# An opening that reads x^T from the host's layout and multiplies both first weight blocks in float32

## What is computed

```python
def rms_norm(x, g, eps=NORM_EPS):
    xf = x.astype(jnp.float32)
    y = xf * lax.rsqrt(jnp.mean(xf * xf, axis=-1, keepdims=True) + eps)
    return (y * g.astype(jnp.float32)).astype(x.dtype)

def swiglu(x, wg, wu, wd):
    return (jax.nn.silu(x @ wg) * (x @ wu)) @ wd

x = x + 0.5 * swiglu(rms_norm(x, ffn1_norm[l]), ffn1_wg[l], ffn1_wu[l], ffn1_wd[l])
```

## Time and profile before

| | |
|---|---|
| median of 3 runs | 858.0 us (857.75 to 858.19) |
| profiled execution | 858.39 us, span of its instructions 856.6 us |
| TensorE busy | 848.3 us, 99% of the span |
| VectorE, ScalarE, GpSimd busy | 637.6, 524.8 and 59.6 us |
| chain that ended last | 98% TensorE |
| mean granted TensorE clock | 0.998 |
| moved by DMA | 162.47 MB, mean 190 GB/s |

### The profile page before, as it was taken

The page is one execution under the profiler, slowest core; times in us unless marked ns, Lnnn a source line. Parts: engine busy times, 40 slices in busy tenths (PEclk is TensorE's granted clock), DMA queues, the critical chain, the costliest instruction groups (busy, mean ns, idle before and its releaser), DMA issues.

```text
span 856.6 us, 11976 instructions
## 1 busy us (share of the span) xinstructions
PE 848.3 (99%) x4775; PEld 738.0 (86%) x4775; DVE 637.6 (74%) x788; ACT 524.8 (61%) x738; POOL 59.6 (7%) x65
## 2 busy tenths in 40 slices
PE   9999999999999999999999999999999999999997
PEld 8988888888889898888888887888888898888885
DVE  5999999987698656765466468758777677877873
ACT  6677777766575544653554356548666665576772
POOL 0022222210000000000000000100000001000001
PEclk9999999999999999999999999999999999999999
DMA  8976566554544655576456545586655655853501
GB/s 271 351 238 201 179 197 197 194 159 158 204 148 141 204 193 177 172 252 231 155 165 231 195 148 187 195 284 224 203 197 193 210 179 168 262 177 108 191 1 50
DMA packets 123991, 162.47 MB, mean 190 GB/s; under 512 B 3864, under 2 KB 111136, under 8 KB 123808
## 3 DMA queue, kind: packets, MB, share of 16 engines
q1 hardware_dynamic: 122320, 154.89, 55.0%
q0 software_dynamic: 1312, 6.29, 2.2%
q10 hardware_dynamic: 304, 0.53, 0.2%
HBM read 160.65 MB, written 1.05 MB: 189 GB/s over the span
## 4 chain that ended last, share of the span: by engine, by line
PE 98%; DVE 1%; ACT 0%; POOL 0%; issue 0%; POOLq 0%; DVEq 0%
PE pAcc L448 23%; PE pG L392 9%; PE pU L392 9%; PE pAcc L392 7%; PE pG L395 5%; PE pR L392 5%; PE pU L395 5%; PE pM L392 4%; PE pAcc L395 3%; PE pR L395 2%; PE pAcc L428 2%; PE pAcc L427 2%; PE pAcc L426 2%; PE pM L395 2%; PE pG L509 1%; PE pM L428 1%
## 5 line engine op out<-in xcount | busy, mean ns | idle before, releaser
L326 DVE TENSOR_TENSOR lo<-raw,hi 128x2048 fp32r<-128x2048 f32 x131 | 298.5, 2288 | 52.7 <-ACT hi L321 52.7
L321 ACT ACTIVATE hi<-raw 128x2048 fp32r<-128x2048 f32 x140 | 265.5, 1907 | 18.4 <-PE pAcc L428 5.6
L392 PE MATMUL pG<-xT,hi 128*128 128x512 f32 x336 | 83.7, 391 | 0.0
L392 PE MATMUL pU<-xT,hi 128*128 128x512 f32 x320 | 80.2, 392 | 0.0
L448 PE MATMUL pAcc<-hi,h_hi 128*128 128x512 f32 x240 | 74.8, 393 | 0.0
L448 PE MATMUL pAcc<-lo,h_hi 128*128 128x512 f32 x240 | 74.2, 390 | 0.0
L448 PE MATMUL pAcc<-hi,h_lo 128*128 128x512 f32 x240 | 74.0, 389 | 0.0
L392 PEld LDWEIGHTS pG<-xT,hi 128*128 128x128 f32 x336 | 62.1, 188 | 13.0 <-issue 0.7
L1110 ACT ACTIVATE h_hi<-h 128x512 fp32r<-128x512 f32 x28 | 17.7, 633 | 81.2 <-PE pAcc L448 75.4
L392 PEld LDWEIGHTS pU<-xT,hi 128*128 128x128 f32 x320 | 57.5, 189 | 10.3
L1629 DVE TENSOR_TENSOR h_lo<-h,h_hi 128x512 fp32r<-128x512 f32 x28 | 19.3, 689 | 46.5 <-ACT h_hi L1110 46.5
(11 more groups left out here) (505 smaller groups left out, 1639.3 us busy)
## 6 DMA issues: line engine op xcount, KB each, us to landing
raw<-in_a_w_in SPq DMA_DIRECT2D x24, 1024.0 KB, 5.3
raw<-in_ffn_wd SPq DMA_DIRECT2D x22, 1024.0 KB, 5.3
raw<-in_ffn_wg SPq DMA_DIRECT2D x21, 1024.0 KB, 5.3
raw<-in_ffn_wu SPq DMA_DIRECT2D x21, 1024.0 KB, 6.2
raw<-in_w_in SPq DMA_DIRECT2D x16, 1024.0 KB, 5.5
raw<-in_a_w_out SPq DMA_DIRECT2D x8, 1024.0 KB, 5.0
raw<-in_w_kv SPq DMA_DIRECT2D x8, 1024.0 KB, 5.5
raw<-in_b_w_qz SPq DMA_DIRECT2D x8, 1024.0 KB, 5.6
```

Of the source, the lines that this page charges most:

```text
L321: act.activation(HI[n % NHL][:, :], RAW[n % NRAW][:, :], ACT.Copy).then_inc(S["hi"], 1)
L326: dve.tensor_tensor(LO[n % NHL][:, :], RAW[n % NRAW][:, :], HI[n % NHL][:, :].bitcast(f32), ALU.subtract).then_inc(S["lo"], 1)
L392: pe.matmul(v3(bank[:, :], 2), wh[:, k, w], x4[:, :, k, :], start=(k == 0), stop=False, skip_group_check=True)
```

## The change

x is no longer transposed by TensorE. The host hands over x^T, features on the partitions, with the gain's 8 columns ahead of it (`x_t`, 128 by 8 + 2048), loaded in four pieces (`load_x_t`). Both first blocks are multiplied in float32 for both tiles; block 1 is not split. ScalarE squares x^T and writes each square 8 elements from the last, so that the 8 chunks of one token and partition are neighbours; VectorE sums these eights (`sum_first`, output 128 x 128), TensorE multiplies the sum with a column of 1/1024 (`mean_square`), and VectorE adds eps (`variance_first`). The rows of x, which the residual needs much later, are loaded by one transfer of 1 MB (`load_x`) ahead of block 8. Tile 1's up product is now unnormed too, so its half of h is multiplied by its power. The small tables for the bias are laid out by the host, and their two transfers stand behind block 3. The core of the diff:

```diff
         def load_block(sp, n):
-            if n >= NRAW:
-                sp.wait_ge(S["lo"], n - NRAW + 1)
-            if n in (NRAW, NRAW + 1):
-                sp.wait_ge(S["used"], 1)
+            if n in (NRAW, NRAW + 1):
+                sp.wait_ge(S["used"], n - NRAW + 1)
+            elif n > NRAW:
+                sp.wait_ge(S["lo"], n - NRAW + 1)
...
+        def load_x_t(engine, b):
+            c = slice(KD + b * 512 if b else 0, KD + (b + 1) * 512)
+            engine.dma_start(XRAW[:, c], T["x_t"][:, c]).then_inc(S[f"x_in{b}"], 16)
+
+        def load_x(sp):
+            sp.wait_ge(S["x_sum"], 2)
+            sp.dma_start(v3(X[:, :], NT), T["x"][0].rearrange("(t p) c -> p t c", p=P)).then_inc(S["x_rows"], 16)
...
+        def mean_square(pe, t):
+            pe.wait_ge(S["x_sum"], t + 1)
+            pe.matmul(VAR[t], SSQ[:, t * P:(t + 1) * P], MEAN, start=True, stop=True).then_inc(S["x_var"], 1)
...
         def pe_start(pe):
-            busy(pe, 7)
-            x_transposes(pe, 0, 0)
-            pe.wait_ge(S["gain0"], 16)
-            pe.transpose(ACC[1][:, 0:KD], G8, IDENT[0:KD, 0:KD]).then_inc(S["gc_ps"], 1)
-            x_transposes(pe, 0, 1)
+            busy(pe, 9)
...
-            pe.wait_ge(S["lo"], 2)
-            pe.wait_ge(S["xt_lo"], 3)
-            to_tokens(pe, 1, U, XT, (1,), half_way=4).then_inc(S["used"], 1)
+            first_block(pe, 1, U, 1, range(0, KD)).then_inc(S["used"], 1)
+            pe.wait_ge(S["xt_lo"], 4)
...
         def xt_first(dve, b):
-            dve.wait_ge(S["xt_ps"], b + 1)
-            dve.tensor_tensor(xf(b), v3(XBANK[b][:, :], 4), fbc(GC[:, 4 * (b % 2):4 * (b % 2) + 4], P),
+            dve.wait_ge(S["x_in0"], 16)
+            if b:
+                dve.wait_ge(S[f"x_in{b}"], 16)
+            dve.tensor_tensor(xf(b), x_raw(b), fbc(GC[:, 4 * (b % 2):4 * (b % 2) + 4], P),
                               ALU.mult).then_inc(S[f"xf{b}"], 1)
+
+        def squares(t):
+            return XSQ[:, t * D:(t + 1) * D].rearrange("p (c k) -> p c k", k=KD)
+
+        def square_first(act, b):
+            act.wait_ge(S[f"x_in{b}"], 16)
+            half = slice(4 * (b % 2), 4 * (b % 2) + 4)
+            act.activation(squares(b // 2).rearrange("p c k -> p k c")[:, half, :], x_raw(b), ACT.Square).then_inc(S["ssq"], 1)
+
+        def sum_first(dve, t):
+            dve.wait_ge(S["ssq"], 2 * t + 2)
+            dve.tensor_reduce(SSQ[:, t * P:(t + 1) * P], squares(t), AX.X, ALU.add).then_inc(S["x_sum"], 1)
+
+        def variance_first(dve, t):
+            dve.wait_ge(S["x_var"], t + 1)
+            c = RS_COL["norm", 0, t][0]
+            dve.tensor_scalar(ST[:, c:c + 1], VAR[t], 1e-6, None, ALU.add).then_inc(S["var"], 1)
...
-                        dve.tensor_tensor(H[:, BC:512], U[:, BC:512], SA[:, BC:512], ALU.mult).then_inc(S["h"], 1)
+                        k = RS_COL["norm", 0, 1][0]
+                        dve.scalar_tensor_tensor(out=H[:, BC:512], in0=U[:, BC:512], scalar=ST[:, k:k + 1], in1=SA[:, BC:512],
+                                                 op0=ALU.mult, op1=ALU.mult).then_inc(S["h"], 1)
...
-                if b == ("ffn1", "gate", 3):
+                if b == ("ffn1", "gate", 2):
+                    load_x(sp)
+                elif b == ("ffn1", "gate", 3):
```

More of the change, by code:

```diff
@@ L57 @@
 NRAW, NHL = 4, 4
+UNSPLIT = 2
 LEAD = 3
@@ L101 @@
     "hi": "hi parts of weight blocks", "lo": "lo parts of weight blocks", "used": "weight blocks multiplied",
-    "x_in00": "x of token tile 0 loaded, its first half", "x_in01": "its second half",
-    "x_in10": "x of token tile 1 loaded, its first half", "x_in11": "its second half",
+    "x_in0": "x^T of token tile 0 loaded, its first half", "x_in1": "its second half",
+    "x_in2": "x^T of token tile 1 loaded, its first half", "x_in3": "its second half",
+    "x_sum": "squares of a token tile summed over the chunks of features",
+    "x_var": "and over the features of a chunk", "x_rows": "x loaded", "mean": "1 / D",
     "first0": "first half of weight block 0 loaded", "first1": "first half of weight block 1 loaded",
@@ L106 @@
     "xf2": "that of token tile 1, first half", "xf3": "its second half",
-    "gc_ps": "first gain by features in a bank", "gc": "and in SBUF", "rb": "powers of the first norm along columns",
-    "hi_first": "hi part of the first half of block 1",
+    "rb": "powers of the first norm along columns",
     "const_in": "lambda vectors, subln gain and DFT matrices loaded",
@@ L296, in load_half @@
                 full[n] if half else S[f"first{n}"], 16)
[L300 to L314, removed]
         def hi(act, n):
@@ L511, in first_block @@
             return end
[L513 to L519, removed]
         def power_row(pe, t):
@@ L1045, in rows @@
             dve.wait_ge(S["rsqrt"], RS_ORDER.index(what) + 1)
-            dve.wait_ge(S[f"gain{g % 2}"], 16 * (g // 2 + 1))
+            dve.wait_ge(S[f"gain{g % 2}"], 16 * (g // 2 + g % 2))
             for n in range(2):
@@ L1631, in dve_turn @@
         def dve_turn(dve, r, g, q, ph, scale, x, n):
+            if r == 0:
+                dve.wait_ge(S["x_rows"], 16)
             lo_half(dve, n + 1, 0)
@@ L2508, in _ @@
             pool.memset(HALF[:, :], -0.5).then_inc(S["half"], 1)
+            pool.memset(MEAN, 1.0 / D).then_inc(S["mean"], 1)
             pool.wait_ge(S["ident"], 1)
@@ L2512, in _ @@
             pool.wait_ge(S["half"], 1)
+            pool.wait_ge(S["mean"], 1)
             power(pool, ("norm", 0, 0))
@@ L2541, in _ @@
         def _(act):
-            load_x(act, 0, 1)
-            load_gain_first(act)
+            load_x_t(act, 1)
             act.wait_ge(S["half"], 1)
             warm(act, ACT.Square)
[L2546 to L2549, removed]
+            for b in range(4):
+                square_first(act, b)
+            warm(act, ACT.Silu)
             xt_hi_first(act, 0)
             xt_hi_first(act, 1)
-            hi_half(act, 0)
-            hi_half(act, 1)
-            warm(act, ACT.Silu)
             xt_hi_first(act, 2)
@@ L2605, in _ @@
             pe.wait_ge(S["ident"], 2)
+            pe.wait_ge(S["mean"], 1)
             pe_ffn(pe, "ffn1", 0, 1)
@@ L2626 @@
     arrays["dft_tok"] = np.ascontiguousarray(dft.transpose(1, 0, 2)).astype(np.float32)
-    arrays["steps"] = 0.5 - np.array(STEPS, np.float32)
+    x_t = arrays["x"][0].reshape(NT, P, KD, P).transpose(3, 0, 2, 1).reshape(P, NT * D)
+    arrays["x_t"] = np.concatenate([arrays.pop("ffn1_norm")[0].reshape(KD, P).T, x_t], axis=1)
+    positions = arrays.pop("positions")[0]
+    arrays["bias_positions"] = np.concatenate([np.tile(positions, (P, 1)), positions.reshape(NT, P).T], axis=1)
+    tables = np.concatenate([0.5 - np.array(STEPS, np.float32), arrays.pop("rel_bias").reshape(-1)])
+    arrays["bias_tables"] = np.tile(tables, (P, 1))
     parts = [arrays.pop(name).reshape(AW // BC, BC) for name in ("a_ln_g_2", "a_ln_b_2", "a_b_s_2")]
```

83 lines of the change are left out of this document (38 added, 45 removed).

## The result

The changed kernel takes 859.26 us, median of 11 runs, against 858.13 for the kernel before (11 runs): ratio 1.0024, 95% interval 1.0017 to 1.0032. By the medians it is slower by 1.1 us (1.0013), by the means of the runs (860.16 against 858.04) by 2.1; the ratio is near that of the means. No change was forecast. Its runs lie in two groups: six from 859.14 to 859.26, five from 860.6 to 862.3. The profiled execution, 860.89 us, is one of the second group; both groups are needed to understand it.

A forecast was written before the change was run, and what follows sets the result against it. TensorE, 98% of the chain, was taken as the bound; the opening's 0.97 us lead is lost to clock and block 2's lo chain, summing to 0.0 us; TensorE's possible 0.3 gain pulls slightly: 857.9 us, range 856.4 to 859.3.

The forecast's parts named there:

- The bytes ahead of it are the same, but for 32 a row: Opening: block 0's first half still lands at 5.87, so the first product starts at 5.95, 0.97 us sooner than 6.92.
- Rival 2: Opening: slower loads from x^T rows 8224 bytes apart keep the first product at 6.92; +0.45 us, 858.4, chance 0.17.
- The clock: TensorE's clock rises at 7.35 as before, taking 0.48 us of the lead; ends no loss, or half a microsecond more.
- the half speed after 5.95: First products: 1.4 us of them run at half speed until 7.35, losing 0.69 us; before, 0.21.
- The working behind the landing: From first product at 5.95 to block 2: power rows at 12.07 and 15.0, block 2 at 21.5 against 21.52.
- lo of block 2: VectorE's rebuilt chain from the second power row ends at 21.4 and holds block 2 until 21.5.
- TensorE alone: Without waiting for block 2's lo part, TensorE would begin block 2 at 21.2, a gain of 0.3 us.
- Mean squares: Two added TensorE products ahead of the power rows, 0.25 us each; ends 0.2 and 0.43.
- rival 3: ScalarE's scattered squares take 3.8 us each instead of 0.63, delaying power row 2: +7.9 us, 865.9; chance 0.09.
- The powers: GpSimd's powers take 0.55 us, ready at 11.3 and 14.4 for rows at 12.07 and 15.0; without that cover lo moves.
- The rows of x: Extra 1 MB load puts block 8 back by 2.8 us, hidden by 3.6 us of cover before its hi.
- Slower: Chance 0.07 of a result slower by over 0.2%, against 0.84 within 0.2% and 0.09 faster.

The follow-up runs named there:

- e4: Kernel before with x padded by 8 columns in HBM: rows 4128 bytes apart, pieces off 256-byte boundaries; 858.20 us, ratio to before 1.0000.
- e6: Changed kernel with 64 columns of zeros between gain and x^T: rows 8480 bytes apart, pieces 32 bytes off; 858.19 us, 1.0005 of before.
- e1: Changed kernel with 56 columns of zeros between gain and x^T: rows 8448 bytes apart, pieces on 256-byte multiples; 858.05 us, 1.0000 of before.
- e2: Changed kernel with x^T in HBM as four arrays, each piece contiguous; 858.41 us, 1.0007 of before.
- e7: e1 with ScalarE's hi and VectorE's lo of block 2 moved ahead of the splits of x^T's tile 1; 857.69 us, 1.0002 of before.
- e8: e1 with squares written with unit step and summed by VectorE over a step of 128 elements; 858.29 us, 1.0009 of before.
- f2: Changed kernel with x^T created first of the arrays in HBM, same program on the chip; 858.08 us, 1.0005 of before.
- e11: e1 without the 1 MB transfer of x in rows and its wait, residual starting from the squares; 858.03 us, 1.0004 of before.
- e9: e7 with 11 fillers (products of the identity at the start) instead of 9; median 858.09 us.
- e10: e7 with 10 fillers and x^T's second piece behind the first half of block 0 on SyncE's queue; 858.58 us.
- f1: Changed kernel with 128 rows of zeros, which nothing reads, appended to x^T in HBM; 859.32 us, 1.0022 of before.

## Why the prediction was wrong

- **"The bytes ahead of it are the same, but for 32 a row": the step that failed.** The prediction took the landing of block 0's first half from the earlier trace rows as a matter of bytes, 5.87 us. It came at 7.29, since the rate up to 5 us was 184 GB/s and not 289: x^T's place in HBM and its row pitch together slow the same bytes. Why they do is open. Rival 2 had the rows 8224 bytes apart, half of this condition, but its price (+0.45) was taken from a first product that stays at 6.92, and not from one that comes later than before; the reason it gave, pieces off 256-byte boundaries, is refuted by e4 and e6.
- **The clock.** The prediction let it rise or not rise, and did not let it fall. The end of its fillers at 5.55 was safe with weights at 5.95; with weights at 7.3 TensorE had no product for 2.1 us, and five of 11 runs are of the long group. Its estimate of the half speed after 5.95, 0.69 us, is one case of several: against 3.69 at full speed, the 16 records take 3.94 us in the profile of e1, 4.41 in that of e2 (0.72 more), and 3.69 in those of e7, e8 and f2.
- **The working behind the landing was right.** e1 has the landings that were assumed. First product 6.09 (5.95 predicted), power rows 11.82 and 14.74 (12.07 and 15.0), lo of block 2 done at 21.19 (21.4), block 2 at 21.30 (21.5), and the time 858.05 against a forecast of 857.9. Part of that nearness is luck: the first product came 0.14 later than forecast, while the slow clock (0.25 for 0.69) and the mean squares cost less. That the lo part holds block 2 was shown by e7, which took it away: block 2 came 0.65 us earlier and the median fell by 0.36. It also shows that TensorE alone would start block 2 at 20.65, not at 21.2.
- **The median, 859.26,** still lies in the range, at its edge. That is luck too: no rival described this opening.
- **Mean squares** were taken at 0.25 us with ends 0.2 and 0.43; they cost 0.12 in the chain, below both:

```profile
12.81 0.12 PE pAcc L513 x2
```

- **The squares (rival 3)** were forecast at 0.63 and took 1.14. The step of 32 bytes costs 1.8 times a plain square, not the 3.8 us of the rival; 1.83 us, from which it would have decided, is not reached.
- **The powers.** GpSimd's second power took 1.05 us and not 0.55. In e1 it ended at 14.61 for the row at 14.74: the cover of 0.4 us shrank to 0.1, and held.
- **The rows of x.** That 3.6 us of cover outlasts a delay of 2.8 was judged right, if with less to spare, 0.4 us and not 0.8: block 8 landed at 32.49 + 9.4 = 41.9, and its hi began at 42.29; e11 shows no price.
- **Chances.** Slower had 0.07, all from the squares. The lateness of the first loads, whatever its cause, should have had a case of its own: everything forecast hung on one landing time.

## What to carry to other kernels

When a change makes the first product wait for transfers alone, its landing times must be measured again, since equal bytes from another array need not come equally fast; where they come late, try another creation order or another row pitch first, for neither touches the program. Keep TensorE supplied until the weights land and no longer: too few fillers risk the clock (13 against 9 took away all runs above 860), too many hold up the first product (e9, e10). And with an operand moved up, look for the next one that the same product waits for: here the lo part of block 2 took most of what the opening gained.

## What the runs showed of the hardware

- The same program with one array created elsewhere in HBM differs by 1.2 us in 860 (changed kernel and f2; f1 agrees with the former), all of it before the first product (7.29 in f1, 6.18 in f2), at a nearly equal busy share of the transfer engines up to 5 us (0.77 and 0.80) and 183 against 269 GB/s.
- TensorE's granted clock fell after 2.1 us without a product: its fillers had ended at full speed, records were at 379 ns until 8.2 us, then 0.56 of 2.4 GHz from 8 to 10 us, mostly the lower level, 1.2 GHz. After 1.7 us in the profile of f1 it did not fall.
- Until its first change in a profile the column of the granted clock says 1.00, though in the profile before a transpose took 421 ns at 4.7 us and 272 at 10.8, which is the low level. At the start of a program the durations are to be read, not the column.
- A ScalarE activation of 128x512 float32 takes 0.63 us with unit step and 1.14 with 32 bytes from one result to the next; a VectorE sum of 1024 float32 takes 1.22 us over neighbours and 1.90 over a step of 512 bytes. Two records of a float32 product with one moving column take 0.12 us.
